# A transformer's last stage: result loads issued before the overflow branch, and half of the token blocks scaled by ScalarE and added by Pool

## The chip, the cores and the metric

The program runs on one core of a Trainium2 chip (trn2). The metric is the device time of one execution in microseconds, as the median of three executions. The core has five engines with instruction streams of their own, which meet only through semaphores: TensorE (PE), VectorE (DVE), ScalarE (ACT), GpSimd (Pool) and SyncE (SP). SyncE computes nothing; here it issues most of the DMA transfers between DRAM and the on-chip memory SBUF. PSUM is the memory into which TensorE writes.

## The reference

A sequence of 512 tokens of width 1024 goes through two blocks: a two-layer transformer with stick-breaking and sliding-window attention, and a hybrid layer (state-space scan, sparse attention, and a hierarchical mixture of experts). The change concerns only how the last block ends. Each token goes to the two best experts of one group; their results are weighted and added to the residual, and the sum is normed:

```
    for e in range(N_EXPERTS):
        he = jax.nn.silu(t @ w_g[e]) * (t @ w_u[e])
        out = out + combine[:, e:e + 1] * (he @ w_d[e])
...
    h = h + gate2 * _hier_moe(hn2, ...)
...
    return _rmsnorm(h, final_g)
```

So for one token the output is (h + w1 * r1 + w2 * r2), divided by its root mean square and multiplied by final_g, where r1 and r2 are the gated results of its two experts.

## The kernel before

The tokens are cut into TB = 4 blocks of 128, one token on each partition, with D = 1024 float32 values each. The kernel is a row of stages. Each stage is a block with one instruction stream per engine, and at its end all engines meet (drain, then semaphores) before the next stage begins.

**The expert stage** (method moe, begun in nsa_end, whose block opens at line 2862) handles the experts in 16 pairs. Pool gathers token rows, TensorE multiplies, VectorE multiplies the result by the gate row (line 3407), and Pool stores each pair's 128 result rows to their places in the DRAM tensor "results" by an indirect DMA (line 3441). That tensor has 2 x 512 rows: the first result of each token, then the second. When all stores have landed (line 3225), SyncE issues the two loads of block 0 (line 3226, by load_results, whose DMA is line 3482): the first results go to the tile first (expert_first in the trace) and the second results to the tile second (w_raw in the trace). Pool waits for the same stores at line 3444.

**The overflow branch** (line 3840) reads the value "passes" from SBUF on every engine. It is positive only when some expert received more tokens than it has slots. Here it is zero, and the code of rest_rows, moe_rest and renew is jumped over. If it ran, it would use the same tiles, which is why renew loads block 0 once more.

**The last stage** (combine, its meeting is line 3494, its branch line 3503):

- SyncE issues the six loads of blocks 1 to 3 (line 3506, DMA line 3482), then stores each finished block (line 3509).
- VectorE runs add(0), add(1), norm(0), add(2), norm(1), add(3), norm(2), norm(3). add(t) is two operations over 128x1024, each with two SBUF operands: first * weight + token (line 3525) and second * weight + first (line 3527). norm(t) turns the sum of squares into a mean (line 3531), waits for ScalarE's root, takes the reciprocal (line 3533) and writes first * that * gain row to the tile second (line 3535); the gain row is read from PSUM.
- ScalarE loads its function table, and for each block squares and sums (line 3517) and takes the root (line 3519).
- Pool clears the semaphores of the stage before and is done.

The tokens themselves (x_tok, nsa_gate in the trace) and the weights (place_w) have been in SBUF since the expert stage.

Of the kernel before, what the change touches and what calls it, by code (L numbers as in the profile page):

```python
# [11 lines left out]
ACT = mybir.ActivationFunctionType  # L12
# [4 lines left out]
TB, KC = S // P, D // P  # L17
# [243 lines left out]
class Kernel:  # L261
# [25 lines left out]
    def sb(self, name, shape, dt=F32):  # L287
        return self.ctx.enter_context(self.nc.sbuf_tensor(name, shape, dt))
# [1081 lines left out]
NP_ = NE // 2  # L1370
# [1485 lines left out]
class Whole(SsmTail):  # L2856
# [342 lines left out]
    def moe(self, st, stage_sem, passed):  # L3199
        nc, d = self.nc, self.d  # L3200
        XR, YR = TB, 4
        sem = lambda what: stage_sem(f"moe_{what}")
# [4 lines left out]
        x_landed, y_stored = self.x_landed, self.y_stored  # L3207
# [11 lines left out]
        def sync(sp):  # L3219
            for n in range(PLACES, len(STEPS)):  # L3220
                kind, i = STEPS[n - PLACES]
                sp.wait_ge((gate_done, up_done, down_done)[kind], i + 1)
                self.issue_step(sp, n)
            for i in range(YR):
                sp.wait_ge(y_stored[i], 16 * (NP_ // YR))
            self.load_results(sp, 0, self.results_landed)

        def tensor(pe):
            def turn(i):
# [198 lines left out]
        def gpsimd(pool):  # L3428
            def gather(i):
                pool.wait_ge(placed, i - 1)  # L3430
                if i >= XR:
                    pool.wait_ge(x_turned_high, i - XR + 1)
                self.gather(pool, i)

            gather(2)
            gather(3)
            for i in range(NP_):
                if i + 4 < NP_:
                    gather(i + 4)
                pool.wait_ge(y_ready, i + 1)  # L3440
                pool.indirect_dma_start(d["results"], bass.IndirectOffsetOnAxis(ap=self.to_row[:, i:i + 1], axis=0), y[:, i % YR], None,
                                        bounds_check=2 * S - 1, oob_is_err=False).then_inc(y_stored[i % YR], 16)
            for i in range(YR):
                pool.wait_ge(y_stored[i], 16 * (NP_ // YR))

        return sync, tensor, scalar, vector, gpsimd


# [43 lines left out]
    def combine(self):  # L3492
        nc = self.nc
        with ExitStack() as st:
            sem, clear = self.stages.open("combine", st)
            weighted, summed, squared, mean, root, inverse, made, out_done = (sem(x) for x in (
                "weighted", "summed", "squared", "mean", "root", "inverse", "made", "out_done"))
            sb = lambda nm, s: st.enter_context(nc.sbuf_tensor(nm, s, F32))
            sq, rs = sb("fin_sq", [P, 2, D]), sb("fin_rs", [P, TB])
            first, second, x_tok, landed = self.first, self.second, self.h_tok, self.results_landed  # L3500
            block = st.enter_context(nc.Block())

            @block.sync  # L3503
            def _(sp):
                for t in range(1, TB):
                    self.load_results(sp, t, landed)
                for t in range(TB):
                    sp.wait_ge(made, t + 1)
                    sp.dma_start(self.out[0, t * P:(t + 1) * P, :], second[:, t]).then_inc(out_done, 16)
                sp.wait_ge(out_done, 16 * TB)  # L3510

            @block.scalar
            def _(act):
                act.preload_act_table_set(SQRT)
                for t in range(TB):
                    act.wait_ge(summed, t + 1)
                    act.activation(sq[:, t % 2], first[:, t], ACT.Square, accum_out=rs[:, t:t + 1]).then_inc(squared, 1)
                    act.wait_ge(mean, t + 1)
                    act.activation(rs[:, t:t + 1], rs[:, t:t + 1], ACT.Sqrt).then_inc(root, 1)  # L3519

            @block.vector
            def _(dve):
                def add(t):
                    dve.wait_ge(landed[t], 32)
                    dve.scalar_tensor_tensor(first[:, t], first[:, t], self.place_w[:, 0, t:t + 1], x_tok[:, t], ALU.mult, ALU.add).then_inc(weighted, 1)  # L3525
                    dve.wait_ge(weighted, t + 1)
                    dve.scalar_tensor_tensor(first[:, t], second[:, t], self.place_w[:, 1, t:t + 1], first[:, t], ALU.mult, ALU.add).then_inc(summed, 1)  # L3527

                def norm(t):
                    dve.wait_ge(squared, t + 1)  # L3530
                    dve.tensor_scalar(rs[:, t:t + 1], rs[:, t:t + 1], 1.0 / D, EPS, ALU.mult, ALU.add).then_inc(mean, 1)  # L3531
                    dve.wait_ge(root, t + 1)
                    dve.reciprocal(rs[:, t:t + 1], rs[:, t:t + 1]).then_inc(inverse, 1)  # L3533
                    dve.wait_ge(inverse, t + 1)
                    dve.scalar_tensor_tensor(second[:, t], first[:, t], rs[:, t:t + 1], self.flat(2, D), ALU.mult, ALU.mult).then_inc(made, 1)  # L3535

                add(0)
                for t in range(1, TB):
                    add(t)
                    norm(t - 1)  # L3540
                norm(TB - 1)

            @block.gpsimd
            def _(pool):
                pool.sem_clear(clear)

    def rest_rows(self):
        nc = self.nc  # L3550
        h_hi, h_lo = self.h
        with ExitStack() as st:
            sem, clear = self.stages.open("rest_rows", st)
            spread, spread_over, steps, normed, rounded, low = (sem(x) for x in ("spread", "spread_over", "steps", "normed", "rounded", "low"))
            sb = lambda nm, s: st.enter_context(nc.sbuf_tensor(nm, s, F32))
            dg, rs, tmp = sb("rows_diag", [P, TB, P]), sb("rows_rs", [P, S]), sb("rows_tmp", [P, 2, S])
            block = st.enter_context(nc.Block())

            @block.sync
            def _(sp):  # L3560

                sp.wait_ge(self.results_landed[0], 32)
                sp.wait_ge(low, KC)

            @block.tensor
            def _(pe):
                pe.wait_ge(spread, TB)
                pe.matmul(self.ps[:, 0, :], self.c("ones"), dg[:].rearrange("p t n -> p (t n)"), start=True, stop=True).then_inc(spread_over, 1)

            @block.scalar  # L3570
            def _(act):
                for k in range(KC):
                    act.wait_ge(normed, k + 1)
                    act.activation(h_hi[:, k, :], tmp[:, k % 2], ACT.Copy).then_inc(rounded, 1)

            @block.vector
            def _(dve):
                link = Link(dve, steps)
                for t in range(TB):
                    dve.tensor_scalar(dg[:, t], self.c("ident"), self.rs_tok[:, t:t + 1], None, ALU.mult).then_inc(spread, 1)  # L3580
                dve.wait_ge(spread_over, 1)
                link(dve.tensor_copy(rs[:], self.ps[:, 0, :]))
                for k in range(KC):
                    part = tmp[:, k % 2]
                    if k >= 2:
                        dve.wait_ge(low, k - 1)
                    link(dve.scalar_tensor_tensor(part, self.x[:, k, :], self.p2("g2", k, 1), rs[:], ALU.mult, ALU.mult))
                    dve.tensor_scalar(part, part, self.p2("ada", 3 * KC + k, 1), None, ALU.add).then_inc(normed, 1)
                    dve.wait_ge(rounded, k + 1)
                    dve.tensor_tensor(h_lo[:, k, :], part, h_hi[:, k, :].bitcast(F32), ALU.subtract).then_inc(low, 1)  # L3590

            @block.gpsimd
            def _(pool):
                pool.sem_clear(clear)
# [128 lines left out]
    def renew(self):  # L3723
        nc = self.nc
        with ExitStack() as st:
            sem, clear = self.stages.open("renew", st)
            turned, taken = sem("turned"), sem("taken")
            landed = [sem("landed")]
            block = st.enter_context(nc.Block())

            @block.sync
            def _(sp):
                self.load_results(sp, 0, landed)
                sp.wait_ge(landed[0], 32)

            @block.tensor
            def _(pe):
# [143 lines left out]
```

## Time and profile before

| | us |
|---|---|
| median of 3 runs | 2678.59 (2678.06 to 2681.99) |
| the profiled execution's own time | 2676.73 |
| its span, first to last instruction | 2674.8 |
| TensorE busy | 2517.3 (94%) |
| VectorE busy | 1477.4 (55%) |
| ScalarE busy | 997.3 (37%) |
| Pool busy | 330.9 (12%) |

All times of the trace count from the first instruction. The first column of a timeline row is the start, the second the duration, both in us; what stands in brackets is how long the engine was idle before it and what ended that. A trailing q (SPq, DVEq) marks an instruction of the engine's sequencer, which waits, branches, drains or issues. The time "to landing" of a DMA counts from its issue to the update of its semaphore. The result stage and what comes before it are the last 30 us of the trace.

### The profile page before, as it was taken

Reading aid. Unit: us, or ns where it says so; the run is one execution under the profiler, and the core shown is the slowest. Engines: PE = TensorE matmul, PEld = TensorE weight load, DVE = VectorE, ACT = ScalarE, POOL = GpSimd, SP = SyncE. Lnnn points to the kernel's source line nnn. Section 1 sums busy time; section 2 is a strip of 40 time slices with the busy share of each in tenths; the row PEclk is TensorE's granted clock in tenths of the full one; section 3 lists DMA queues with packets and bytes.
Section 4 is the critical chain, followed back from the end, with each engine's and each line's share of the span. In section 5 each row is a group of like instructions: output and inputs, shape, how many; then the busy total and the mean of one; then the engine's idle time right before and its main releaser. Section 6 shows DMA issues by size and latency. Waiting matters only on the chain. (4 is left out here: it accounts for less than half of the span.)

```text
span 2674.8 us, 33667 instructions
## 1 busy us (share of the span) xinstructions
PE 2517.3 (94%) x13581; PEld 1982.7 (74%) x13581; DVE 1477.4 (55%) x2202; ACT 997.3 (37%) x1412; POOL 330.9 (12%) x187
## 2 busy tenths in 40 slices
PE   8999999999999999999999999998999797979974
PEld 7777788888887778888887887777778565866542
DVE  4564456544646535545545765775864887455313
ACT  4246533322333555422222334334521587321112
POOL 0000004431500000135523000001000000001110
PEclk9999999999999999999999999999999899989997
DMA  4221133443322212424443234444343002369996
GB/s 152 82 72 55 63 113 124 143 143 119 110 88 82 64 56 71 142 95 142 143 141 94 79 93 134 135 134 144 122 152 110 17 2 80 97 246 394 424 425 242
DMA packets 265027, 355.99 MB, mean 133 GB/s; under 512 B 33444, under 2 KB 238756, under 8 KB 252196
## 3 DMA queue, kind: packets, MB, share of 16 engines
q1 hardware_dynamic: 256452, 333.30, 36.9%
q0 software_dynamic: 8320, 20.46, 2.1%
q8 instruction: 110, 1.80, 0.3%
q14 instruction: 49, 0.40, 0.1%
q10 hardware_dynamic: 96, 0.02, 0.0%
HBM read 337.38 MB, written 24.19 MB: 135 GB/s over the span
## 5 line engine op out<-in xcount | busy, mean ns | idle before, releaser
L210 PE MATMUL ps<-h_hi,w_hi 128*128 128x512 f32 (+1 forms) x1736 | 698.4, 402 | 22.0 <-DVE room L879 4.3
L212 PE MATMUL ps<-h_hi,w_lo 128*128 128x512 f32 (+1 forms) x1736 | 680.7, 392 | 0.0
L211 PE MATMUL ps<-h_lo,w_hi 128*128 128x512 f32 (+1 forms) x1736 | 680.4, 392 | 0.0
L187 ACT ACTIVATE w_hi<-w_raw 128x2048 fp32r<-128x2048 f32 (+1 forms) x168 | 316.8, 1886 | 742.8 <-PE ps L212 728.4
L192 DVE TENSOR_TENSOR w_lo<-w_raw,w_hi 128x2048 fp32r<-128x2048 f32 (+1 forms) x168 | 392.0, 2333 | 177.1 <-ACT w_hi L187 176.9
L210 PEld LDWEIGHTS ps<-h_hi,w_hi 128*128 128x128 f32 (+1 forms) x1736 | 328.7, 189 | 102.7 <-issue 35.6
L211 PEld LDWEIGHTS ps<-h_lo,w_hi 128*128 128x128 f32 (+1 forms) x1736 | 328.8, 189 | 70.0 <-issue 4.1
L212 PEld LDWEIGHTS ps<-h_hi,w_lo 128*128 128x128 f32 (+1 forms) x1736 | 328.0, 189 | 71.0
L210 PE MATMUL ps<-merged_hi,w_hi 128*128 128x512 f32 x640 | 249.8, 390 | 0.0
L212 PE MATMUL ps<-merged_hi,w_lo 128*128 128x512 f32 x640 | 249.1, 389 | 0.0
L211 PE MATMUL ps<-merged_lo,w_hi 128*128 128x512 f32 x640 | 249.0, 389 | 0.0
L1343 POOL TENSOR_TENSOR room<-room,silu_c 128x2048 f32<-128x2048 f32 x24 | 119.8, 4990 | 940.2 <-DMA room<-in_w_ada 940.2
L1271 DVE TENSOR_TENSOR x<-x,ps 128x1024 f32<-128x1024 f32 x38 | 46.4, 1222 | 224.2 <-PE ps L212 224.2
L212 PEld LDWEIGHTS ps<-merged_hi,w_lo 128*128 128x128 f32 x640 | 120.1, 188 | 25.1
L210 PEld LDWEIGHTS ps<-merged_hi,w_hi 128*128 128x128 f32 x640 | 120.2, 188 | 24.7
L211 PEld LDWEIGHTS ps<-merged_lo,w_hi 128*128 128x128 f32 x640 | 120.2, 188 | 24.6
L1346 POOL TENSOR_TENSOR room<-room 128x1024 f32<-128x1024 f32 (+1 forms) x48 | 115.6, 2408 | 3.8
L1289 DVE TENSOR_TENSOR merged_lo<-room,merged_hi 128x1024 fp32r<-128x1024 f32 x32 | 115.6, 3613 | 0.0
L879 DVE SCALAR_TENSOR_TENSOR room<-ps,x_rs 128x512 f32<-128x512 f32 x58 | 40.1, 691 | 134.2 <-PE ps L212 127.4
L1285 DVE SCALAR_TENSOR_TENSOR room<-ps,room 128x1024 f32<-128x1024 f32 x32 | 39.2, 1224 | 78.3 <-PE ps L212 78.1
L2818 ACT ACTIVATE nsa_p<-nsa_p,nsa_mx 128x512 f32<-128x512 f32 (+3 forms) x128 | 70.8, 554 | 18.8 <-DVE nsa_mx L2769 17.2
L3330 ACT ACTIVATE moe_silu<-ps 128x256 f32<-128x256 f32 x16 | 6.1, 383 | 171.6 <-PE ps L3259 171.6
(488 smaller groups left out, 3538.6 us busy)
## 6 DMA issues: line engine op xcount, KB each, us to landing
w_raw<-in_w_in SPq DMA_DIRECT2D x268, 256.0 KB, 3.6
w_raw<-in_w_up SPq DMA_DIRECT2D x128, 256.0 KB, 3.5
w_raw<-in_w_down SPq DMA_DIRECT2D x128, 256.0 KB, 3.7
room<-in_w_ada SPq DMA_DIRECT2D x96, 256.0 KB, 6.0
expert_over_h<-in_w_exp_down SPq DMA_DIRECT2D x10, 1024.0 KB, 25.2
w_raw<-in_w_out SPq DMA_DIRECT2D x32, 256.0 KB, 3.5
ssd_e<-chunk_decays SPq DMA_DIRECT2D x32, 256.0 KB, 4.1
w_raw<-in_w_ssm_out SPq DMA_DIRECT2D x32, 256.0 KB, 3.6
```

Of the source, the lines that this page charges most:

```text
L187: act.activation(self.hi[:, q, :, 0:cols], raw[:, q, :, 0:cols], ACT.Copy).then_inc(self.hi_ready, 1)
L192: dve.tensor_tensor(self.lo[:, q, :, 0:cols], raw[:, q, :, 0:cols], self.hi[:, q, :, 0:cols].bitcast(F32), ALU.subtract).then_inc(self.lo_ ...
L210: pe.matmul(out, w[0], x[0], start=start, stop=False)
L211: pe.matmul(out, w[0], x[1], start=False, stop=False)
L212: return pe.matmul(out, w[1], x[0], start=False, stop=stop)
L879: dve.scalar_tensor_tensor(kept(t, c), bank(t, c), factor, x_rs[:], ALU.mult, ALU.mult).then_inc(taken0 if c == 0 and t != T_SWK else W.ev ...
L1271: dve.tensor_tensor(two(self.x, t), two(self.x, t), self.pst[:, q, 0:n, :], ALU.add).then_inc(W.evicted[q], 1)
L1285: dve.scalar_tensor_tensor(r[:, q], self.pst[:, q, 0:n, :], 0.0, rs.unsqueeze(1).to_broadcast([P, n, S]), ALU.max, ALU.mult).then_inc(W.ev ...
L1289: dve.tensor_tensor(two(u[1], t), r[:, q], two(u[0], t).bitcast(F32), ALU.subtract).then_inc(u_low, 1)
L1343: pool.tensor_tensor(w, w, c, ALU.mult).then_inc(ada_step, 1)
L1346: pool.tensor_tensor(w[:, 0:half], w[:, 0:half], w[:, half:2 * half], ALU.add).then_inc(ada_step, 1)
L2818: act.activation(p[:, i, e, 0:W], p[:, i, e, 0:W], ACT.Exp, bias=mx[:, i, e:e + 1], scale=-1.0, accum_out=den[:, i, e:e + 1]).then_inc(exp ...
```

## The change

In the expert stage, SyncE issues the loads of all four blocks behind its wait for the stores, and Pool no longer waits for the stores. In combine, SyncE issues no load. Blocks 0 and 1 are added as before. For blocks 2 and 3, ScalarE multiplies first by its weight (both blocks, placed behind block 0's root and ahead of block 1's square), Pool adds the token rows, and VectorE does only the second operation. In the overflow path, which is not taken here, the waits and the renewed loads cover all four blocks.

```diff
--- before.py
+++ after.py
@@ -3223,7 +3223,8 @@
                 self.issue_step(sp, n)
             for i in range(YR):
                 sp.wait_ge(y_stored[i], 16 * (NP_ // YR))
-            self.load_results(sp, 0, self.results_landed)
+            for t in range(TB):
+                self.load_results(sp, t, self.results_landed)
 
         def tensor(pe):
             def turn(i):
@@ -3440,8 +3441,6 @@
                 pool.wait_ge(y_ready, i + 1)
                 pool.indirect_dma_start(d["results"], bass.IndirectOffsetOnAxis(ap=self.to_row[:, i:i + 1], axis=0), y[:, i % YR], None,
                                         bounds_check=2 * S - 1, oob_is_err=False).then_inc(y_stored[i % YR], 16)
-            for i in range(YR):
-                pool.wait_ge(y_stored[i], 16 * (NP_ // YR))
 
         return sync, tensor, scalar, vector, gpsimd
 
@@ -3493,8 +3492,8 @@
         nc = self.nc
         with ExitStack() as st:
             sem, clear = self.stages.open("combine", st)
-            weighted, summed, squared, mean, root, inverse, made, out_done = (sem(x) for x in (
-                "weighted", "summed", "squared", "mean", "root", "inverse", "made", "out_done"))
+            weighted, summed, squared, mean, root, inverse, made, out_done, scaled, joined = (sem(x) for x in (
+                "weighted", "summed", "squared", "mean", "root", "inverse", "made", "out_done", "scaled", "joined"))
             sb = lambda nm, s: st.enter_context(nc.sbuf_tensor(nm, s, F32))
             sq, rs = sb("fin_sq", [P, 2, D]), sb("fin_rs", [P, TB])
             first, second, x_tok, landed = self.first, self.second, self.h_tok, self.results_landed
@@ -3502,8 +3501,6 @@
 
             @block.sync
             def _(sp):
-                for t in range(1, TB):
-                    self.load_results(sp, t, landed)
                 for t in range(TB):
                     sp.wait_ge(made, t + 1)
                     sp.dma_start(self.out[0, t * P:(t + 1) * P, :], second[:, t]).then_inc(out_done, 16)
@@ -3512,7 +3509,15 @@
             @block.scalar
             def _(act):
                 act.preload_act_table_set(SQRT)
+
+                def scale(t):
+                    act.wait_ge(landed[t], 32)
+                    act.activation(first[:, t], first[:, t], ACT.Copy, scale=self.place_w[:, 0, t:t + 1]).then_inc(scaled, 1)
+
                 for t in range(TB):
+                    if t == 1:
+                        scale(2)
+                        scale(3)
                     act.wait_ge(summed, t + 1)
                     act.activation(sq[:, t % 2], first[:, t], ACT.Square, accum_out=rs[:, t:t + 1]).then_inc(squared, 1)
                     act.wait_ge(mean, t + 1)
@@ -3522,8 +3527,11 @@
             def _(dve):
                 def add(t):
                     dve.wait_ge(landed[t], 32)
-                    dve.scalar_tensor_tensor(first[:, t], first[:, t], self.place_w[:, 0, t:t + 1], x_tok[:, t], ALU.mult, ALU.add).then_inc(weighted, 1)
-                    dve.wait_ge(weighted, t + 1)
+                    if t < 2:
+                        dve.scalar_tensor_tensor(first[:, t], first[:, t], self.place_w[:, 0, t:t + 1], x_tok[:, t], ALU.mult, ALU.add).then_inc(weighted, 1)
+                        dve.wait_ge(weighted, t + 1)
+                    else:
+                        dve.wait_ge(joined, t - 1)
                     dve.scalar_tensor_tensor(first[:, t], second[:, t], self.place_w[:, 1, t:t + 1], first[:, t], ALU.mult, ALU.add).then_inc(summed, 1)
 
                 def norm(t):
@@ -3543,6 +3551,9 @@
             @block.gpsimd
             def _(pool):
                 pool.sem_clear(clear)
+                for t in range(2, TB):
+                    pool.wait_ge(scaled, t - 1)
+                    pool.tensor_tensor(first[:, t], first[:, t], x_tok[:, t], ALU.add).then_inc(joined, 1)
 
 
 
@@ -3559,7 +3570,8 @@
             @block.sync
             def _(sp):
 
-                sp.wait_ge(self.results_landed[0], 32)
+                for t in range(TB):
+                    sp.wait_ge(self.results_landed[t], 32)
                 sp.wait_ge(low, KC)
 
             @block.tensor
@@ -3725,13 +3737,14 @@
         with ExitStack() as st:
             sem, clear = self.stages.open("renew", st)
             turned, taken = sem("turned"), sem("taken")
-            landed = [sem("landed")]
+            landed = [sem("landed")] * TB
             block = st.enter_context(nc.Block())
 
             @block.sync
             def _(sp):
-                self.load_results(sp, 0, landed)
-                sp.wait_ge(landed[0], 32)
+                for t in range(TB):
+                    self.load_results(sp, t, landed)
+                sp.wait_ge(landed[0], 32 * TB)
 
             @block.tensor
             def _(pe):
```

## Rows read from the trace of the kernel before

**Rows 1.** The page, section 1: busy time, share and instructions of each engine

```profile
PE 2517.3 (94%) x13581; PEld 1982.7 (74%) x13581; DVE 1477.4 (55%) x2202; ACT 997.3 (37%) x1412; POOL 330.9 (12%) x187
```

**Rows 2.** The chain of waits, last 30 us: start us, us, what

```profile
2649.71 7.13 DMA w_raw<-token_results
```

**Rows 3.** Timeline of VectorE, last stage

```profile
2652.69 1.28 DVE L3525 SCALAR_TENSOR_TENSOR expert_first<-expert_first,place_weight,nsa_gate 128x1024 f32<-128x1024 f32 x1 [11.88 <-issue]
...
2656.87 1.29 DVE L3525 SCALAR_TENSOR_TENSOR expert_first<-expert_first,place_weight,nsa_gate 128x1024 f32<-128x1024 f32 x1 [1.57 <-DMA w_raw<-token_results]
...
2661.20 1.28 DVE L3525 SCALAR_TENSOR_TENSOR expert_first<-expert_first,place_weight,nsa_gate 128x1024 f32<-128x1024 f32 x1
...
2663.72 0.15 DVE L3531 TENSOR_SCALAR fin_rs<-fin_rs 128x1 f32<-128x1 f32 x1
2664.14 0.16 DVE L3533 RECIPROCAL fin_rs<-fin_rs 128x1 f32<-128x1 f32 x1 [0.27 <-ACT fin_rs L3519]
2664.34 1.28 DVE L3535 SCALAR_TENSOR_TENSOR w_raw<-expert_first,fin_rs,ps 128x1024 f32<-128x1024 f32 x1
2665.53 1.28 DVE L3525 SCALAR_TENSOR_TENSOR expert_first<-expert_first,place_weight,nsa_gate 128x1024 f32<-128x1024 f32 x1
...
2670.48 1.28 DVE L3535 SCALAR_TENSOR_TENSOR w_raw<-expert_first,fin_rs,ps 128x1024 f32<-128x1024 f32 x1
```

**Rows 4.** Timeline of SyncE, from the last store on

```profile
2644.91 0.33 SPq L3482 DMA_DIRECT2D expert_first<-token_results  x1
...
2649.71 1.80 SPq L3482 DMA_DIRECT2D w_raw<-token_results  x1
2651.56 0.43 SPq L3482 DMA_DIRECT2D expert_first<-token_results  x1
2652.03 0.43 SPq L3482 DMA_DIRECT2D w_raw<-token_results  x1
...
2652.98 1.38 SPq L3482 DMA_DIRECT2D w_raw<-token_results  x1
```

**Rows 5.** The meeting's line 2862: durations min/median/max in ns, first and last start

```profile
L2862 POOLq DRAIN  x1: 2660/2660/2660, 2645.1 to 2645.1; - x1
L2862 SPq DRAIN  x1: 122/122/122, 2645.8 to 2645.8; - x1
L2862 SPq EVENT_SEMAPHORE  x1: 17/17/17, 2647.9 to 2647.9; - x1
```

**Rows 6.** Line 3503, same columns: the jump

```profile
L3503 DVEq COMPARE_BRANCH  x1: 72/72/72, 2648.6 to 2648.6; - x1
L3503 PEldq COMPARE_BRANCH  x1: 3855/3855/3855, 2648.6 to 2648.6; - x1
```

**Rows 7.** Windows: us, busy of each engine (operations), clock, DMA share, GB/s

```profile
2646.50:2649.00 2.50, 0.00 (x0) 0.00 (x0) 0.00 (x0) 0.06 (x1) 0.00 (x0) 0.50 0.96 364
```

**Rows 8.** Line 1072, columns as in rows 5: issues of another group of loads

```profile
L1072 SPq DMA_DIRECT2D room<-in_w_ada x96: 428/470/2213, 394.1 to 1389.4; - x96
```

**Rows 9.** Timeline of Pool: its last store of results

```profile
2641.59 0.98 POOL L3441 DMA_INDIRECT token_results<-results,to_row  x1 [4.08 <-DVE results L3407]
```

**Rows 10.** DMA issues, window of block 0's second load: KB each, us to landing

```profile
w_raw<-token_results SPq DMA_DIRECT2D x1, 512.0 KB, 4.7
```

**Rows 11.** Timeline of ScalarE, last stage

```profile
2663.90 0.20 ACT L3519 ACTIVATE fin_rs<-fin_rs 128x1 f32<-128x1 f32 x1 [3.09 <-DVE fin_rs L3531]
2664.01 1.04 ACT L3517 ACTIVATE fin_sq<-expert_first 128x1024 f32<-128x1024 f32 x1
```

**Rows 12.** Timeline of Pool in two earlier stretches

```profile
596.27 3.26 POOL L1346 TENSOR_TENSOR room<-room 128x1024 f32<-128x1024 f32 x1
...
1148.58 4.58 POOL L1343 TENSOR_TENSOR room<-room,silu_c 128x2048 f32<-128x2048 f32 x1
1153.24 2.40 POOL L1346 TENSOR_TENSOR room<-room 128x1024 f32<-128x1024 f32 x1
```

**Rows 13.** Line 1289, columns as in rows 5: an operation with two SBUF operands

```profile
L1289 DVE TENSOR_TENSOR merged_lo<-room,merged_hi x32: 1218/4622/4630, 410.0 to 1424.3; 128x1024 fp32r<-128x1024 f32 x32
```

## The prediction

> **What bounds the kernel now.** I first read the busy shares of the page: TensorE is busy for 94% of the span and the whole rest of the kernel is untouched by this diff [rows 1]. Only the last 30 us can move, so everything below is about the stretch from 2644.85 us, when the last expert result has been stored, to the end at 2674.8 us. There TensorE has nothing left to do.
>
> The second view is the chain of waits. In this stretch it goes from SyncE's second load of block 1 straight to VectorE: the load is issued at 2649.71 and is under way for 7.13 us, and from 2656.87 on the chain stays on VectorE [rows 2]. The third is VectorE's own timeline. Its first operation of the last stage starts at 2652.69 after 11.88 us of idle time that the profile puts down to "issue", the second block starts after a wait of 1.57 us for the load, and from then on there is no gap: one block takes 4.33 us (2661.20 to 2665.53) [rows 3].
>
> The "issue" label is worth opening, because block 0's data was there long before. SyncE began its two loads at 2644.91 [rows 4]. Then all engines meet at the end of the expert stage: SyncE arrives at 2645.8, but Pool, whose DRAIN runs 2.66 us from 2645.1, holds the meeting until about 2647.8, and SyncE goes on at 2647.92 [rows 5]. Next comes the branch around the overflow work. TensorE's branch instruction takes 3855 ns; VectorE's is 72 ns but its next instruction starts only at 2652.69, 4.0 us later [rows 6, 3]. I read both as the same thing: after the jump the engine's instructions have to be brought in. So block 0 is limited by meeting plus jump (4.77 us from 2647.92 to 2652.69), block 1 by its load, and blocks 2 and 3 by VectorE.
>
> **The change part by part.** All sums are against the profiled execution, span 2674.8 us, whose own time was 2676.73 us; the median of the three runs is 2678.59, 1.86 us above it. I apply the difference in span to the median.
>
> *Block 1's wait goes.* Loads of blocks 1 to 3 are now issued right behind those of block 0. After a start-up the queue moves 364 GB/s [rows 7]. Eight loads of 0.524 MB from 2646.5 at that rate put blocks 0 and 1 in place by 2652.3 and all of them by 2658.0. Block 1 is wanted only 2.52 us after VectorE starts, about 2656.5, and block 3 at about 2660.3 (below). So the delay of block 1 disappears: it started at 2656.87 where 2652.69 + 2.52 = 2655.21 was possible, a gain of 1.66 us. What covers the rest of the loading is the meeting and the jump; without them VectorE would wait for data again.
>
> *SyncE reaches the meeting later.* This is the price, and six issues are what is moved past it. An issue with room costs 0.33 to 0.43 us, with a pitch of 0.47 (2651.56 to 2652.03) [rows 4]. Eight of them from 2644.91: 0.37 for the first, then seven at 0.48, end near 2648.6; SyncE's DRAIN of 0.12 [rows 5] and the release put the meeting at 2648.9 instead of 2647.92, which is +1.0. From below: with every issue at the shortest 0.33 plus 0.05 it ends at 2647.95, +0.3 with the DRAIN and the release. From above: two of the six moved issues took 1.80 and 1.38 us [rows 4], 2.3 us more than the usual; if that comes along, it is +3.3. Of 96 loads of another kind the median is 0.47 and the longest 2.21 [rows 8], so long ones are the exception; I take +1.0.
>
> *Pool's wait goes.* Pool no longer waits for the stores, so its DRAIN can begin behind its last issue, which ends at 2642.6 [rows 9], instead of at 2645.1 [rows 5]. With the same 2.66 us it is over by 2645.4, and even if it lasts until its old 2647.8 SyncE is later. Worth nothing by itself, because SyncE takes its place as the last to arrive; without the issues it would have been worth up to 2 us. That is why the first part doesn't pay twice.
>
> *The jump.* It costs VectorE 4.0 us with a DMA queue that is nearly empty when it begins. Now it falls into the middle of the result loads. From below it costs nothing more. From above I take what crowding did to a result load: 7.13 us for block 1's second load [rows 2] against 4.7 for block 0's [rows 10], +2.4; a gain is excluded, since nothing gets less crowded. The instructions are few bytes beside 4.19 MB, so I stay near the low end: +0.3.
>
> *The split of blocks 2 and 3.* VectorE loses one operation of 1.28 us in each, 1.32 with the step to the next [rows 3], together 2.64 us. What replaces it lies on a longer path: ScalarE scales, Pool adds, and only then does VectorE add the second result. I lay it out from VectorE's first operation, T. Blocks 0 and 1 are added until T+5.04, the mean of block 0 follows, ScalarE's root at T+5.22 (0.18 later), and VectorE's output operation runs from T+5.66 and lets the next one in at T+6.85 [rows 3]. ScalarE reaches the scaling of block 2 only behind that root, 0.11 later, at T+5.33, because the diff puts it there in program order. A 128x1024 operation takes it 1.04 us [rows 11], so block 2 is scaled at T+6.38 and block 3 at T+7.3; the square of block 1 waits behind both and is done by T+8.5, in time. Pool's add is not in this trace's tail. Its nearest rows are the same operation in the same shape elsewhere: 2.40 us at 1153.24, where VectorE beside it ran only an operation that reads PSUM, and 3.26 at 596.27, where VectorE had one with two SBUF operands waiting [rows 12]. Beside VectorE's output operation, which reads PSUM, I take 2.40: block 2 joined at T+8.82. VectorE was free at T+6.85, so it idles 2.0 us, which alone gives back most of the 2.64.
>
> Then the two engines collide. At T+8.86 VectorE wants its second add, with both operands in SBUF, and Pool wants to begin block 3, both at the same moment. A VectorE operation with two SBUF operands takes 1.2 us at best and 4.62 in the median of the rows beside Pool's work [rows 13]; the 3.26 of Pool is 2.40 plus most of such an operation. They take turns. VectorE answers ScalarE's root 0.04 us after its end (2663.90 + 0.20 to 2664.14) [rows 3, 11], while Pool's own instructions follow each other at 0.08 us (1148.58 + 4.58 to 1153.24) [rows 12]. So I let VectorE go first: Pool's block 3 runs from T+10.14 to T+12.54; VectorE does norm 1 until T+11.87, waits 0.7, adds block 3 at T+12.58, and its last output operation starts at T+14.40 for block 2 and T+16.21 for block 3. Before, it started at T+17.79 (2670.48). That contains the 1.66 of block 1, so this whole stage goes from 17.79 to 16.21, −1.58, of which the split itself costs 0.08. The bounds: with no collision the last operation starts at T+15.50, −2.29; with Pool going first at T+17.95, +0.16.
>
> The Trainium skill bears on this twice. "SBUF — State Buffer", section "SBUF: two separate sides", says that a VectorE instruction with two SBUF inputs and a GpSimd one that reads SBUF lock each other out for the whole instruction; by that rule one of the two waits in full, and the 4.62 us in the trace agree. "GPSIMD Engine Reference", section "Engine selection", advises VectorE for elementwise adds because GpSimd is about twice as slow; the trace agrees with 2.40 us against 1.28, and by it alone the split would be dropped, which by my own layout would change the sum by −0.08.
>
> *The end* stays: the last store, its landing and the closing meeting are as before. The stores of blocks 2 and 3 are now 1.81 us apart, and 0.524 MB at 364 GB/s take 1.4, so they hardly meet.
>
> **The sum:** +1.0 (meeting) + 0.3 (jump) − 1.58 (stage) = −0.3 us. Span 2674.5, profiled time about 2676.4, median 2678.59 − 0.3 = 2678.3 us.
>
> **The rivals.** (1) *Pool goes first.* Pool starts block 3 before VectorE's second add and VectorE stands still for 2.4 us. Stage +0.16, sum +1.5, time 2680.1. For it: Pool's next instruction is already queued with its condition met. Against it: the 0.04 us reaction of VectorE. Chance 0.20. (2) *No collision.* If scalar_tensor_tensor with two SBUF operands does not take turns with Pool (only tensor_tensor is shown to), the stage gains 2.29 and the sum is −1.0, time 2677.6. Chance 0.15. (3) *The front of the tail becomes the bound.* SyncE's eight issues stall as two did before (+3.3) and the jump is crowded (+2.4). Added to the stage's −1.58 that is +4.1, 2682.7; together with Pool first +5.9, 2684.4. It decides against the change as soon as SyncE arrives more than 1.3 us after the old meeting. For it: the stalls came at exactly these loads. Against it: 0.47 in the median of 96 others [rows 8]. It ends slower than before. Chance 0.12. (4) *The change doesn't do what it says:* early loads don't help because VectorE starts block 1 late for another reason. Then the 1.66 stays, sum +1.4, 2679.9. Chance 0.03. The forecast case has 0.50.
>
> **How the numbers follow.** A measurement of this kernel can tell some 0.2%, 5.4 us, from no change; the runs of before spread from 2678.06 to 2681.99. No case reaches −5.4: the largest gain, no collision with the cheapest meeting and jump, is −2.0. Only the worst of rival 3 passes +5.4. With the scatter of the runs added I give faster 0.03, same 0.91, slower 0.06. The range goes from 2675.8 (the −2.0 and a little scatter) to 2682.3 (most of rival 3's weight left out).
>
> **What would show it.** SyncE's eight issues from 2644.9 without a break, ending near 2648.6, and its EVENT_SEMAPHORE at the stage's end near 2648.9; Pool's DRAIN beginning before 2643. VectorE's first operation near 2654.0 and its fourth with no wait behind the second. Then a VectorE wait of 2 us on Pool in front of block 2 and one of 0.7 in front of block 3, with Pool's two adds at 2.4 and 3.7 us. If VectorE's second add of block 2 shows 3.7 us instead, Pool went first; if all adds are plain, there was no collision. The forecast is wrong in kind if VectorE starts before 2652.7 or after 2657.

## The result, and the profile after

The changed kernel takes 2687.13 us (median of 20 executions, 2677.47 to 2691.38) against 2680.49 us for the kernel before (median of 20, 2676.52 to 2686.92). The medians lie 6.6 us apart. The ratio estimated from all executions is 1.0020, with a 95% interval from 1.0013 to 1.0027, that is +5.4 us (+3.5 to +7.2). The forecast was 2678.3 us in a range from 2675.8 to 2682.3, and no change that can be told; the measured time is above the range. The profiled execution of the changed kernel took 2677.82 us, with a span of 2675.9 us, only 1.1 us more than before.

That last number hides the loss. Two of the 20 executions, the profiled one among them, took 2677.5 and 2677.8 us at a mean granted clock of 0.978; the other eighteen took 2684.3 to 2691.4 us at 0.968 to 0.973. No run shows why those two got more clock. Up to SyncE's first result load the two programs do the same, yet in the twelve traces of this study that load begins anywhere between 2642.3 and 2656.1 us. The granted clock of TensorE in the stages ahead differs from execution to execution: the stage that ends at the meeting of line 2669 took 170.6 us at a mean of 0.99 in the changed kernel's trace and 176.1 us at 0.89 in that of pool_wait_only, with the same code. In the changed kernel's first trace that load began 2.6 us earlier than before. So everything below is measured from that load, and I call the time from it to the end of the span **the tail**: 2674.8 − 2644.9 = 29.9 us before [rows 4], 33.6 us in the changed kernel. In a second trace of the same changed kernel it was 34.2 us. The tail has four parts: until SyncE leaves the meeting; the jump, until VectorE's first operation; the stage, from that to the start of VectorE's last operation; and the end.

SyncE's timeline in the changed kernel shows the eight loads, none with a long stall:

```profile
2642.34 0.33 SPq L3481 DMA_DIRECT2D expert_first<-token_results  x1
...
2644.13 0.60 SPq L3481 DMA_DIRECT2D expert_first<-token_results  x1
...
2645.80 0.50 SPq L3481 DMA_DIRECT2D w_raw<-token_results  x1
```

The meeting's line (durations in ns, first and last start) answers to [rows 5]. Pool's DRAIN is now over long before SyncE's, which begins 4.0 us after the first load, where it was 0.9:

```profile
L2862 POOLq DRAIN  x1: 4816/4816/4816, 2638.8 to 2638.8; - x1
L2862 SPq DRAIN  x1: 122/122/122, 2646.4 to 2646.4; - x1
L2862 SPq EVENT_SEMAPHORE  x1: 17/17/17, 2646.6 to 2646.6; - x1
```

Pool ends at 2638.8 + 4.8 = 2643.6, SyncE leaves at 2646.6, 4.3 us after its first load, where it was 3.0 before.

The jump (line 3502, same columns) answers to [rows 6]: TensorE's branch takes 6.1 us instead of 3.9.

```profile
L3502 DVEq COMPARE_BRANCH  x1: 72/72/72, 2647.3 to 2647.3; - x1
L3502 PEldq COMPARE_BRANCH  x1: 6055/6055/6055, 2647.3 to 2647.3; - x1
```

VectorE's timeline answers to [rows 3]:

```profile
2653.87 1.28 DVE L3531 SCALAR_TENSOR_TENSOR expert_first<-expert_first,place_weight,nsa_gate 128x1024 f32<-128x1024 f32 x1 [15.63 <-issue]
...
2656.39 1.28 DVE L3531 SCALAR_TENSOR_TENSOR expert_first<-expert_first,place_weight,nsa_gate 128x1024 f32<-128x1024 f32 x1
...
2659.52 1.28 DVE L3543 SCALAR_TENSOR_TENSOR w_raw<-expert_first,fin_rs,ps 128x1024 f32<-128x1024 f32 x1
2662.87 3.27 DVE L3535 SCALAR_TENSOR_TENSOR expert_first<-w_raw,place_weight,expert_first 128x1024 f32<-128x1024 f32 x1 [2.06 <-POOL expert_first L3556]
...
2667.87 1.28 DVE L3535 SCALAR_TENSOR_TENSOR expert_first<-w_raw,place_weight,expert_first 128x1024 f32<-128x1024 f32 x1
...
2671.49 1.28 DVE L3543 SCALAR_TENSOR_TENSOR w_raw<-expert_first,fin_rs,ps 128x1024 f32<-128x1024 f32 x1
```

It starts at 2653.87, 7.25 us after the meeting; before, it was 4.77. Block 1 follows without a gap. Block 2 has two losses: an idle 2.06 us for Pool, and an operation of 3.27 us where all the others of its kind take 1.28. The last operation starts 17.62 us after the first; before, that was 17.79. Pool's two adds show as one row of 4.64 us, starting at 2660.42:

```profile
2660.42 4.64 POOL L3556 TENSOR_TENSOR expert_first<-expert_first,nsa_gate 128x1024 f32<-128x1024 f32 x2 [20.42 <-ACT expert_first L3515]
```

| kernel | meeting | jump | stage | end | tail | time against before |
|---|---|---|---|---|---|---|
| before | 3.0 | 4.8 | 17.8 | 4.3 | 29.9 | 1 |
| changed | 4.3 | 7.2 | 17.6 | 4.5 | 33.6 | 1.0020 (1.0013 to 1.0027) |
| changed_again | 4.5 | 7.5 | 17.6 | 4.5 | 34.2 | 1.0013 (1.0004 to 1.0022) |
| loads_only | 4.2 | 7.2 | 16.1 | 4.4 | 32.0 | 1.0009 (1.0000 to 1.0018) |
| split_only | 3.0 | 4.8 | 18.6 | 4.3 | 30.6 | 1.0004 (0.9995 to 1.0013) |
| pool_wait_only | 1.4 | 5.7 | 16.1 | 4.3 | 27.5 | 0.9993 (0.9984 to 1.0002) |
| pool_wait_again | 1.4 | 5.8 | 16.1 | 4.3 | 27.7 | 0.9993 (0.9985 to 1.0002) |
| two_early | 2.1 | 6.9 | 16.1 | 4.3 | 29.5 | 0.9997 (0.9987 to 1.0006) |
| quarter_loads | 4.0 | 4.8 | 16.1 | 4.4 | 29.3 | one execution |
| pool_second | 4.5 | 7.4 | 16.5 | 4.5 | 32.9 | 1.0011 (1.0002 to 1.0021) |
| gated_split | 1.4 | 5.4 | 16.8 | 4.3 | 27.9 | 0.9989 (0.9980 to 0.9999) |
| split_own_waits | 1.4 | 5.4 | 15.3 | 4.3 | 26.4 | 0.9992 (0.9983 to 1.0001) |

All parts are in us. They come from one trace each; in the two kernels that were traced twice the tails came out 0.6 and 0.2 us apart. The times have intervals 4 to 5 us wide. Where I compare kernels by a microsecond, I use the tails. By time alone only changed, changed_again, pool_second and gated_split can be told from the kernel before; for the others the times don't contradict the tails, and no more.

### The profile page after: what moved, and what is told of

Its sections match the earlier page's. It is cut to its first block and busy times, and to the rows that moved or that the text cites. A ratio compares the mean times of both kernels' runs of the same rounds, so it can differ in the third digit from the quotient of the medians.

```text
span 2675.9 us, 33668 instructions
## 1 busy us (share of the span) xinstructions
PE 2511.2 (94%) x13581; PEld 1979.1 (74%) x13581; DVE 1473.8 (55%) x2200; ACT 999.3 (37%) x1414; POOL 336.2 (13%) x189
```

## The experiments

**The changed kernel again.** The same code, run a second time.

> The changed kernel as it is, to see how much of its trace and of its time comes back. Tail here means the time from SyncE's first result load to the end of the span: 29.9 us in the kernel before, 33.6 in the changed one. Theory A (the whole loss is in the tail: meeting +1.3, jump +2.5, split +1.5, block 1's wait -1.7): tail 33.6 within 0.5, and a timed difference to the kernel before of +3.5 to +4. Theory B (part of the measured +5 to +6 us is elsewhere, for instance in TensorE's granted clock): the tail is again 33.6 but the timed difference is 5 us or more, with the granted clock lower than in the kernel before.

The tail was 34.2 us, just outside the 33.6 within 0.5 that theory A expected, and the time 1.0013 of the kernel before, +3.5 us (+1.1 to +5.9), which is theory A's. Theory B's 5 or more lies inside that interval too. The first measurement's interval, +3.5 to +7.2, also holds the tail's +3.7 to +4.3. So a loss outside the tail isn't shown, and it isn't excluded either: 1 us more or less can't be told here. Meeting and jump were each 0.3 us longer than in the first trace; that is how far two traces of one kernel can differ.

**The two halves of the change.** loads_only takes the changed kernel and gives all additions back to VectorE:

```diff
-                    if t == 1:
-                        scale(2)
-                        scale(3)
...
-                    if t < 2:
+                    if True:
...
-                for t in range(2, TB):
-                    pool.wait_ge(scaled, t - 1)
-                    pool.tensor_tensor(first[:, t], first[:, t], x_tok[:, t], ALU.add).then_inc(joined, 1)
```

> The eight early loads and Pool's missing wait, but VectorE adds all four blocks as before. Theory A: meeting at 4.3 us after the first load, jump 7.2 us instead of 4.8, stage 16.1 us from VectorE's first operation to its last, tail 29.9 + 1.3 + 2.5 - 1.7 = 32.0, timed +2.1. Rival (it was the split that delayed VectorE's start, by the longer code of the stage): jump 4.8, tail 29.5, timed -0.4. Theory B: timed difference far above the tail's.

Meeting 4.2, jump 7.2, stage 16.1, tail 32.0: what theory A expected in every part. The jump rows and VectorE's timeline:

```profile
L3502 DVEq COMPARE_BRANCH  x1: 72/72/72, 2661.0 to 2661.0; - x1
L3502 PEldq COMPARE_BRANCH  x1: 6215/6215/6215, 2661.0 to 2661.0; - x1
```

```profile
2667.51 1.28 DVE L3528 SCALAR_TENSOR_TENSOR expert_first<-expert_first,place_weight,nsa_gate 128x1024 f32<-128x1024 f32 x1 [15.47 <-issue]
...
2670.03 1.28 DVE L3528 SCALAR_TENSOR_TENSOR expert_first<-expert_first,place_weight,nsa_gate 128x1024 f32<-128x1024 f32 x1
...
2683.63 1.28 DVE L3540 SCALAR_TENSOR_TENSOR w_raw<-expert_first,fin_rs,ps 128x1024 f32<-128x1024 f32 x1
```

With the code of the stage as it was before, VectorE still starts late. The rival that blamed the longer code falls.

split_only keeps the split and puts the loads of blocks 1 to 3 and Pool's wait back where they were:

```diff
-            for t in range(TB):
-                self.load_results(sp, t, self.results_landed)
+            self.load_results(sp, 0, self.results_landed)
...
+            for i in range(YR):
+                pool.wait_ge(y_stored[i], 16 * (NP_ // YR))
...
+                for t in range(1, TB):
+                    self.load_results(sp, t, landed)
```

> The split of blocks 2 and 3 over ScalarE and Pool, but SyncE loads blocks 1 to 3 behind the jump and Pool waits for the stores as before. Theory A: meeting and jump as before (3.0 and 4.8 us), block 1 1.7 us late, a VectorE add of 3.3 us in block 2 behind Pool's second add, tail 29.9 + 1.5 = 31.4, timed +1.5. Rival (the split is harmless and the front alone costs): tail 29.9, timed 0.

Meeting 3.0 and jump 4.8 are those of the kernel before. VectorE's add of block 2 shows the collision again, with Pool's second add beside it:

```profile
2667.29 3.46 DVE L3538 SCALAR_TENSOR_TENSOR expert_first<-w_raw,place_weight,expert_first 128x1024 f32<-128x1024 f32 x1 [2.66 <-POOL expert_first L3559]
```

```profile
2667.32 2.34 POOL L3559 TENSOR_TENSOR expert_first<-expert_first,nsa_gate 128x1024 f32<-128x1024 f32 x1
```

The tail was 30.6 us, 0.8 less than I expected. Its first wait was smaller: block 1's second load landed 10.4 us after the first issue where the kernel before had 11.9, so 0.1 us was waited for instead of 1.66. ScalarE's scaling of block 2 waited for that block's load, which landed 13.8 us after the first issue, and so began 0.6 us later behind the root than in the changed kernel. Without these waits, and with 3.27 for the 3.46, the stage is the changed kernel's 17.6. Theory A holds in kind: in the tail, the split by itself costs 0.7 us against the kernel before. The time (1.0004) can't tell it from no change.

**Pool's wait alone.** From the kernel before:

```diff
-            for i in range(YR):
-                pool.wait_ge(y_stored[i], 16 * (NP_ // YR))
```

> The kernel before without Pool's wait for the stores, nothing else. Theory A: Pool's DRAIN was the last to arrive, so the meeting comes 1.5 to 1.9 us earlier (1.2 to 1.5 us after SyncE's first load instead of 3.0). If only loads in flight slow the jump, it now falls on block 0's loads and loses up to 1.5 of that: tail 28.2 to 29.7. Rival (Pool's DRAIN waits for its own stores anyway): meeting as before, tail 29.9.

```profile
L2862 POOLq DRAIN  x1: 4820/4820/4820, 2647.9 to 2647.9; - x1
L2862 SPq DRAIN  x1: 123/123/123, 2652.3 to 2652.3; - x1
L2862 SPq EVENT_SEMAPHORE  x1: 17/17/17, 2652.9 to 2652.9; - x1
```

```profile
L3501 PEldq COMPARE_BRANCH  x1: 4495/4495/4495, 2653.6 to 2653.6; - x1
```

SyncE's first load began at 2651.45, so it leaves the meeting after 1.4 us instead of 3.0. The jump costs 5.7 us, 0.9 more than before: it now falls on block 0's loads, as A expected. The tail, 27.5 us, is even below the expected 28.2, because block 1's data is in time as well (stage 16.1). It wasn't the early load that block 1 needed. VectorE now starts 7.1 us after the first load instead of 7.8, but SyncE passes the jump quickly and issues block 1's loads at 2.9 us after the first one instead of 4.4. The same kernel once more, beside the last experiment:

> pool_wait_only once more, beside it on the same chip. Expected: meeting 1.4, jump 5.3 to 5.7, stage 16.1, tail 27.2 to 27.6, timed 2.3 us below the kernel before. If it comes out level with the kernel before, the gain of the first time was scatter.

Tail 27.7 us and the same ratio, 0.9993. The tail is 2.2 to 2.4 us shorter in both traces, a gain of 0.1%. Each of the two intervals of the time still holds 1, so neither time shows it alone.

**How much is in flight at the jump.** two_early puts four loads ahead of the meeting, on top of pool_wait_only:

```diff
-            self.load_results(sp, 0, self.results_landed)
+            for t in range(2):
+                self.load_results(sp, t, self.results_landed)
...
-                for t in range(1, TB):
+                for t in range(2, TB):
```

> No split and no wait of Pool for the stores; SyncE loads blocks 0 and 1 before the meeting and blocks 2 and 3 behind the jump: a dose of four loads, between the two of pool_wait_only (jump 5.7 us) and the eight of loads_only (7.2). Theory A (what is in flight slows the jump): meeting at 2.3 us after the first load, jump about 6.5, stage 16.1, tail 29.3, so 1.8 more than pool_wait_only with its 27.5. Rival (block 1's early data pays for it): tail 27.5 or less.

Meeting 2.1, jump 6.9, tail 29.5: A's numbers within 0.4 us. Two loads more before the meeting cost 1.8 to 1.9 us of tail and bring nothing, since the stage was 16.1 already.

```profile
L3502 PEldq COMPARE_BRANCH  x1: 7015/7015/7015, 2652.9 to 2652.9; - x1
```

quarter_loads is loads_only with all eight issues kept and most of the bytes taken away: it leaves three quarters of each result row unloaded.

```diff
-            sp.dma_start(to[:, t], self.d["results"][i * S + t * P:i * S + t * P + P, :]).then_inc(landed[t], 16)
+            sp.dma_start(to[:, t, 0:D // 4], self.d["results"][i * S + t * P:i * S + t * P + P, 0:D // 4]).then_inc(landed[t], 16)
```

> As loads_only, with all eight issues before the meeting, but each load moves only the first quarter of its columns; the other columns of the results stay what the tiles held, so the output is not the reference's. Theory A (the bytes still queued when the engines jump slow the jump): meeting at 4.2 as in loads_only, jump back to 4.8 to 5.2 us, stage 16.1, tail 29.5 to 29.9. Rival (it is the number of issues, or the later meeting itself): jump 7.2, tail 32.

```profile
L3502 PEldq COMPARE_BRANCH  x1: 3715/3715/3715, 2654.0 to 2654.0; - x1
```

```profile
2658.15 1.28 DVE L3528 SCALAR_TENSOR_TENSOR expert_first<-expert_first,place_weight,nsa_gate 128x1024 f32<-128x1024 f32 x1 [12.89 <-issue]
...
2660.67 1.28 DVE L3528 SCALAR_TENSOR_TENSOR expert_first<-expert_first,place_weight,nsa_gate 128x1024 f32<-128x1024 f32 x1
```

With the meeting almost as late (4.0) and the number of issues the same, the jump is back at 4.8 us and TensorE's branch at 3.7. At the jump 0.15 MB of loads were still to be moved, where the changed kernel had 2.8. So the issues cost the meeting, and what is still queued costs the jump. This is the experiment that decides. It doesn't separate bytes from packets, of which few were left as well.

The queues of the changed kernel show where the jump's 2.5 us go. Here are the DMA packets by queue (packets, MB, share of the 16 engines) in two windows. From the jump to 2650.0 there are result loads alone, and the fetches of instructions, q14 and q8, come only between 2650 and 2652:

```profile
q1 hardware_dynamic: 289, 1.05, 101.4%
```

```profile
q1 hardware_dynamic: 198, 0.70, 102.9%
q14 instruction: 4, 0.03, 4.0%
q8 instruction: 1, 0.02, 3.2%
```

In the kernel before the same five packets run between 2649.5 and 2650.0, about 1 us after its jump at 2648.6:

```profile
q14 instruction: 4, 0.03, 21.8%
q8 instruction: 1, 0.02, 18.5%
```

They move 0.05 MB in both. Narrower windows put them 1.0 to 1.4 us after the jump before, and 3.5 to 3.9 us after it in the changed kernel (2650.8 to 2651.2). From the last of them to VectorE's first operation it is 2.7 us in both. So what grew is the time from the jump until they run, by 2.5 us, and that is the whole growth of the jump. In pool_wait_only, with 0.76 MB of loads to be moved at the jump, they run 1.7 to 2.2 us after it.

**Who goes first.** pool_second is the changed kernel with one wait more:

```diff
                     pool.wait_ge(scaled, t - 1)
+                    if t == 3:
+                        pool.wait_ge(summed, 3)
```

> The changed kernel, with one more wait: Pool begins block 3's add only when VectorE has finished block 2's second add. Theory A (VectorE's add of 3.3 us is 1.28 of work behind 2.0 of Pool's block 3): the add goes back to 1.3 us, Pool's second add takes 2.35 alone, stage 16.2 to 16.4 instead of 17.6, tail 32.3, or 1.3 less than the changed kernel. Rival (the add is slow because ScalarE's and Pool's results arrive late, whoever goes first): add still above 2 us, stage 17.6.

```profile
2671.34 1.28 DVE L3535 SCALAR_TENSOR_TENSOR expert_first<-w_raw,place_weight,expert_first 128x1024 f32<-128x1024 f32 x1 [2.07 <-POOL expert_first L3558]
...
2675.23 1.28 DVE L3535 SCALAR_TENSOR_TENSOR expert_first<-w_raw,place_weight,expert_first 128x1024 f32<-128x1024 f32 x1 [0.80 <-POOL expert_first L3558]
```

```profile
2668.87 2.36 POOL L3558 TENSOR_TENSOR expert_first<-expert_first,nsa_gate 128x1024 f32<-128x1024 f32 x1 [20.84 <-ACT expert_first L3515]
2672.77 2.36 POOL L3558 TENSOR_TENSOR expert_first<-expert_first,nsa_gate 128x1024 f32<-128x1024 f32 x1 [1.54 <-DVE expert_first L3535]
```

VectorE's add is 1.28 us again, Pool's adds are 2.36 each, and VectorE waits 0.80 us for the second where I had laid out 0.7. The stage is 16.5 us instead of 17.6. The tail is 32.9 against 33.6 and 34.2; it was expected at 32.3, but meeting and jump came out as in changed_again, not as in the first trace. So the add of 3.27 us was an operation of 1.28 standing behind Pool's next add. The stage is still longer than without a split (16.1): in this order of ScalarE's work the split gains nothing even without the collision.

**A split that pays.** gated_split has the split of the changed kernel behind the front of pool_wait_only: the loads of blocks 1 to 3 are back behind the jump. It moves the scaling ahead of the roots, and lets each of Pool's adds begin when VectorE is about to run its output operation, which reads PSUM:

```diff
                 for t in range(TB):
...
                     act.activation(sq[:, t % 2], first[:, t], ACT.Square, accum_out=rs[:, t:t + 1]).then_inc(squared, 1)
+                    if t < 2:
+                        scale(t + 2)
...
                     pool.wait_ge(scaled, t - 1)
+                    pool.wait_ge(summed, t)
```

> What A would build: no wait of Pool for the stores, two early loads only, ScalarE scales block 2 ahead of block 0's root and block 3 ahead of block 1's root, and each add of Pool waits until VectorE's previous add of the same kind is done, so that it runs beside VectorE's output operation, which reads PSUM. Expected: meeting 1.4, jump 5.7, no VectorE add above 1.3 us, stage 15.1 instead of 16.1, tail 26.5, timed 3.4 us below the kernel before. Rival (a split over three engines costs more hand-overs than it saves): stage 16.1 or more, tail 27.5 or more.

The stage was 16.8 us, worse than the rival's 16.1, but not by hand-overs. ScalarE's timeline:

```profile
2664.11 1.15 ACT L3516 ACTIVATE expert_first<-expert_first,place_weight 128x1024 f32<-128x1024 f32 x1 [1.80 <-DMA w_raw<-token_results]
2665.17 0.19 ACT L3524 ACTIVATE fin_rs<-fin_rs 128x1 f32<-128x1 f32 x1
```

The scaling of block 2 waited 1.80 us for the load of w_raw, a tile that it doesn't read: both loads of a block count into one semaphore. Behind it stood block 0's root. split_own_waits gives the two loads semaphores of their own:

```diff
+            firsts = {t: sem(f"first_landed{t}") for t in range(2, TB)}
...
-                    act.wait_ge(landed[t], 32)
+                    act.wait_ge(firsts[t], 16)
```

> As gated_split, but ScalarE's scaling waits only for the load that it reads (a semaphore of its own for the first results of blocks 2 and 3), no longer for the block's second load too. In gated_split that second load landed 12.4 us after the first issue and held ScalarE, which held block 0's root: stage 16.8 against the 15.1 expected. Theory A (only that wait spoiled it; hand-overs to Pool cost 0.6 us of VectorE's time against 1.3 saved): stage 15.0 to 15.3, tail 26.1 to 26.6, timed 3.5 us below the kernel before. Rival (the split doesn't pay even when nothing is late): stage 16.1 or more, tail 27.5 or more.

```profile
2663.45 1.28 DVE L3538 SCALAR_TENSOR_TENSOR expert_first<-w_raw,place_weight,expert_first 128x1024 f32<-128x1024 f32 x1 [0.81 <-POOL expert_first L3560]
...
2667.34 1.28 DVE L3538 SCALAR_TENSOR_TENSOR expert_first<-w_raw,place_weight,expert_first 128x1024 f32<-128x1024 f32 x1 [0.80 <-POOL expert_first L3560]
...
2670.97 1.28 DVE L3546 SCALAR_TENSOR_TENSOR w_raw<-expert_first,fin_rs,ps 128x1024 f32<-128x1024 f32 x1
```

```profile
2660.99 2.36 POOL L3560 TENSOR_TENSOR expert_first<-expert_first,nsa_gate 128x1024 f32<-128x1024 f32 x1 [14.42 <-DVE expert_first L3538]
2664.88 2.36 POOL L3560 TENSOR_TENSOR expert_first<-expert_first,nsa_gate 128x1024 f32<-128x1024 f32 x1 [1.54 <-DVE expert_first L3538]
```

The stage was 15.3 us and the tail 26.4, as A expected: 3.5 us below the kernel before and 7.2 below the changed one. VectorE waits 0.8 us for Pool in each block and saves an operation of 1.32. By the time it is 0.9992 (0.9983 to 1.0001) of the kernel before, 3.3 us in the medians (2678.70 against 2682.02). It has the shortest tail of all, but the time doesn't confirm its place: its lead over pool_wait_again, 1.6 us in the medians, is inside the intervals, and gated_split, with a tail 1.5 us longer, has the lower ratio, 0.9989.

## Why the prediction was wrong

**The reading of the tail** was right: meeting, jump, block 1's load and VectorE are its parts, and each moved as a part of its own.

**The meeting**, +1.0 forecast: +1.3, or +1.5 in the repeat. The last early issue ended 4.0 us after the first one began, where I had laid out 3.7: they took 0.33 to 0.60 us, none stalled. The upper bound was built on the stalls of 1.80 and 1.38 us [rows 4]; in the twelve traces such issues stand only behind the jump (pool_wait_only has one of 1.50 us there), and no early one took more than 0.89. Pool's DRAIN was rightly priced at nothing as long as SyncE is later. Its worth without the issues, "up to 2 us", measured 1.6.

**Block 1's wait**, −1.66: gone, as forecast. But pool_wait_only loses it too, without any early load. I had called the loads' cover the meeting and the jump and never asked what a shorter meeting alone would do for them.

**The jump**, +0.3 forecast, is the first step that failed: it measured +2.5, a little above even the upper bound of +2.4. I argued from bytes ("few bytes beside 4.19 MB") where the delay is that of waiting behind what is queued: the fetches ran 3.5 us after the jump instead of 1.0. The sign that I had given, VectorE near 2654.0, was met at 2653.87 by luck, because the first load began 2.6 us earlier in that trace; counted from that load, VectorE started after 11.5 us where I had laid out 9.1. The row nearest to this was the one from which I took the bound, a load that took 2.4 us longer in company, and I should have stayed with it. The Trainium skill, "Runtime: NRT & Kernel Launch", section "Instruction fetch mechanics", says that a taken branch out of the instruction window forces a DMA fetch before execution goes on. That agrees with the jump rows and the q14 and q8 packets; that the fetch waits behind the kernel's own transfers is what these runs add.

**The split**, +0.08 forecast, is the second: it measured 17.6 against 16.1 without a split, +1.5. This is the rival "Pool goes first", laid out with a stage of 17.95 and measured at 17.62. I decided the tie on the wrong row. I took ScalarE's answer time, 0.04 us, for VectorE's wait on Pool. In the changed kernel VectorE's add starts 0.10 us after Pool's first add ends (2660.42 + 2.35 to 2662.87), while Pool's two adds follow each other with no gap at all (4.64 us for two of 2.35). But who starts first by the records doesn't settle it either: in split_only VectorE's add is recorded 0.03 us ahead of Pool's (2667.29 against 2667.32), and still Pool's took its 2.34 us and VectorE's 3.46. Pool went first in all three traces with such a contact; what decides it isn't shown. The layout up to there held: block 2's add was wanted at T+8.86 and came at T+9.00.

**The sum.** With the two steps at their measured sizes it is +1.3 + 2.5 − 1.66 + 1.5 = +3.6 us, and the tail gives +3.7. That combination was in the prediction only as the far corner of rival 3. I had given each bad outcome a small chance of its own, though none of them turned out to be a matter of chance: the crowded jump came back in every trace with four or more early loads, and Pool first in all three with the contact. The chances were therefore wrong too: "slower by over 0.2%" had 0.06, and the measured ratio is at that line. Another 1.9 us of the measured time is the kernel before itself, whose median rose from 2678.59 in three executions to 2680.49 in twenty. Added to those 2678.59, the tail's +3.7 alone gives 2682.3, the upper end of the range. What lies between the tail's +3.7 to +4.3 and the first measurement, +5.4 by the ratio and 6.6 in the medians, stays open.

## What to carry to other kernels

Loads issued ahead of a meeting and a taken branch were not free here although nobody waited for them: the issuing engine arrived later, and the instruction fetches behind the branch came 2.5 us later, behind loads that were still queued. Count them there, and look for the engine that really holds the meeting; here deleting one wait took 2.2 to 2.4 us off the tail, and the six early loads put more than that back (32.0 in loads_only against 27.5). When work moves to a second engine that contends with the first, lay out the order of the two at the moment of contact and fix it with a wait if the wrong order costs; and let each wait cover only the data that its instruction reads.

## What the runs showed of the hardware

- After this taken branch VectorE and TensorE stood still for about 4 us in the kernel before, SyncE, ScalarE and Pool for 0.4 to 0.5. With two early loads still in flight at the jump the meeting-to-VectorE time was 5.4 to 5.8 us, with four or eight early loads 6.9 to 7.5, with eight loads of a quarter of the bytes 4.8. That four loads cost almost as much as eight fits where the fetches stand: in the changed kernel and in two_early alike they began 3.5 to 3.7 us after the jump, when another 1.4 MB of loads had been moved. In the changed kernel 1.4 MB of loads still followed, so the fetches didn't wait for the whole queue. What sets that amount isn't shown.
- Pool's DRAIN took 4.81 to 4.82 us where it began together with the indirect store's issue. Begun only after the store had landed, it still took 2.66 us [rows 5].
- VectorE's scalar_tensor_tensor with two SBUF operands and Pool's tensor_tensor run one behind the other: VectorE's took 3.27 and 3.46 us instead of 1.28 where Pool was first (changed kernel, split_only). The Trainium skill, "SBUF — State Buffer", section "SBUF: two separate sides", has this as an exclusive lock, and the trace agrees. Beside VectorE's operation that reads PSUM, Pool's add took 2.36 us and VectorE's 1.28 (split_own_waits).
